# One change in five places of a two-block transformer kernel: the first weights sent by pairs of input tiles, the output projection of the gated-linear layer computed with tokens in rows, residual sums on VectorE, and fewer dummy products

## Chip, core and metric

The kernel runs on one core of a Trainium2 chip. The time is the device time of one execution, in microseconds (us); smaller is better. Engines are named as in the profile: PE is TensorE (the matrix engine), PEld its weight loads, DVE is VectorE, ACT is ScalarE, POOL is GpSimd, SP is the engine that issues the loads.

## What is computed

A sequence of 256 tokens of width 1024, in float32, passes through two blocks. Cut to what matters here:

```
c_act = silu(c)
mod = c_act @ w_ada + b_ada;  sh1, sc1, g1, sh2, sc2, g2 = split(mod, 6)
h = rmsnorm(x, norm_g[0]) * (1 + sc1) + sh1
y = hybrid_mixer(h, w_in, ...)               # 3 small attentions, gates, w_out
x = x + g1 * rmsnorm(y, norm_g[1])           # norm "n2"
h = rmsnorm(x, norm_g[2]) * (1 + sc2) + sh2  # norm "n3"
y = conv_ffn(h)                              # w_up, conv, gelu, w_down
x = x + g2 * rmsnorm(y, norm_g[3])           # norm "n4"

y = gla_mixer(x, ...)                        # gated-linear attention; its last step is  ... @ gla_w_out
x = layer_norm(ALPHA * x + y, ln_g[0], ln_b[0])      # norm "n5"
k, v = shared_kv(x, w_kv)
y = dilated_mixer(x, swa_w_in, swa_w_out, k, v)      # its last step is  ... @ swa_w_out
x = layer_norm(ALPHA * x + y, ln_g[1], ln_b[1])      # the output
```

## The kernel before

**Chunks.** All weights are cut into chunks of 2048 numbers per partition (1 MB; some are smaller), numbered in the order of use: QC, QI, KK, MISC, QA ... VB, ZG (12), BRANCH (3), WOUT (4), UP (22), DOWN (12), GK (2), GA, GQ (2), GV (4), GG (4), GOUT (4), SK (3), SV (3), SWA (16), SOUT (4). GOUT is `gla_w_out`, SK and SV are `w_kv`, SOUT is `swa_w_out`. SP issues the loads in the order of the list `STREAM` into four buffers `raw`; a load waits until the chunk four places ahead of it in the ring is used.

**Splitting.** A float32 product is made of three products in a shorter format (`three`): ACT rounds a chunk to its high part (`high`, whi), DVE subtracts it for the low part (`low`, wlo), and PE multiplies high by high, high by low and low by high. Activations are split in the same way (hhi/hlo, gohi/golo, ohi/olo). A chunk takes 48 such products of 256 columns. The split parts have three slots (`c % SPL`), and results have three PSUM banks (`res`, `bank(r)`); a bank is free when the engine that `drainer_of` names has read it.

**Layout.** Activations lie with features on the partitions and tokens in the columns (8 tiles of 128 features by 256 tokens). `fm` computes a chunk in that layout, `tm` with tokens on the partitions. `fm_first` interleaves two chunks over the input tiles k, so that it can start when the first tile of a freshly made activation is there; it needs the splits of both chunks.

**The start.** The first three chunks (QC, QI, KK) are not split: `direct` multiplies float32 as it is. They are loaded one chunk at a time between the eight parts of `w_ada` that the first norm needs (`ada`: a product and sum on DVE, two instructions for each part). `ADA_FIRST` fixes the order 0, 4, 1, 5, 2, 6, 3, 7. When parts j and 4 + j are done, DVE makes `pcol` for two tiles, ACT makes these two tiles of `tb` (the normed input), and PE may multiply them. The last tiles so wait for part 7. Then ACT splits chunks MISC and QA (`high(DIRECT)`, `high(DIRECT + 1)`), and copies the result QC in four pieces (`swap`); DVE rotates it (`rope`, m_qc), which frees the PSUM bank that chunk MISC needs.

**The norms n2, n3 and n4.** PE multiplies squares by a matrix of 1/1024 (`sums`, `last_squares`: its result is the mean on all partitions). ACT makes a first value of the root (`norm_guess`), for which `load_root` has loaded its table, and DVE improves it (`norm_rstd`) and scales y. The sums x + y go in four pairs of tiles in the order `PAIRS`; the second pair is summed on POOL (`add_pair`), the others on DVE. In n4 the first low part follows the third pair (`low_pair`). Meanwhile PE runs dummy products (`warm(n)`), the last before GK with n = 36.

**Norm n5.** Chunks GOUT to GOUT + 3 are computed by `fm_first` and `fm`, DVE adds the residual `xe` (x times ALPHA in another order of tokens, made early by POOL), PE forms means twice (`shift_mean`, `rest_mean`) and the mean of squares, DVE and ACT make the normed tiles one by one, and `fm_first` multiplies SK and SK + 1.

**The end.** For SOUT the residual is brought in by PE: sixteen products of x with the identity (`residual`), twelve of them before the first product of SOUT; for these PE waits for three free banks. ACT copies each result with a sum over its row (`accum_out`) and then squares it; DVE norms the rows and SP stores them.

## Time and profile before

| | |
|---|---|
| time, median of 3 runs (lowest, highest) | 786.86 us (785.42, 787.11) |
| the profiled execution: its time, its span | 786.95 us, 785.2 us |
| PE busy | 751.5 us, 96% of the span |
| DVE busy | 528.7 us, 67% |
| ACT busy | 394.9 us, 50% |
| POOL busy | 121.3 us, 15% |
| granted PE clock, mean | 0.987 |

The span runs from the first to the last instruction of the profiled execution, and its time holds 1.75 us beside it. Busy PE time counts the dummy products too, so 96% doesn't say that PE did useful work for all of it. In a row of the timeline the first number is the start in us from the span's start, the second how long the row's instructions took together, and in brackets stands how long the engine was idle before it and what ended that. PE records a float32 product as two instructions. In a row of the windows stand the stretch and its length, then the busy us of PE, PEld, DVE, ACT and POOL with the number of instructions in brackets, the granted PE clock (1.00 is the full 2.4 GHz, 0.50 is 1.2 GHz), the share of the DMA engines' time, and GB/s.

### The profile page before, as it was taken

How to read it: one execution, taken by the hardware profiler on the slowest of the kernel's cores; microseconds unless marked ns; L12 is line 12 of the kernel's file. 1: busy time of each engine (PE TensorE's matmuls, PEld its weight loads, DVE VectorE, ACT ScalarE, POOL GpSimd, SP SyncE). 2: the span in 40 equal slices, each digit the busy share in tenths (PEclk: the TensorE clock that was granted, in tenths of full speed). 3: DMA queues.
4: the chain of work that ended last, by engine and by line, in shares of the span. 5: the costliest groups of instructions: out<-in, count | busy, mean ns of one | idle time of the engine just before them, and what ended most of it. 6: DMA issues, size and time to landing. Idle time of an engine off the chain costs nothing. (4 is left out here: it accounts for less than half of the span.)

```text
span 785.2 us, 14371 instructions
## 1 busy us (share of the span) xinstructions
PE 751.5 (96%) x6044; PEld 732.4 (93%) x6044; DVE 528.7 (67%) x770; ACT 394.9 (50%) x555; POOL 121.3 (15%) x100
## 2 busy tenths in 40 slices
PE   8899989999898999999999999999989999999996
PEld 7889889899897999999999999999989999999995
DVE  5879978765868687778656556926685556556544
ACT  4195454555353555454444347627445555555633
POOL 0040000000521100000002150000025655333000
PEclk9999999999999999999999999979999999999999
DMA  8975575464355356554565524523437653333101
GB/s 355 417 291 215 215 268 187 190 259 171 108 177 199 115 208 210 173 200 157 209 247 210 211 90 180 184 88 108 145 124 246 201 185 135 134 109 119 44 1 54
DMA packets 20954, 140.10 MB, mean 178 GB/s; under 512 B 2357, under 2 KB 2997, under 8 KB 4890
## 3 DMA queue, kind: packets, MB, share of 16 engines
q1 hardware_dynamic: 20458, 137.28, 48.2%
q0 software_dynamic: 432, 1.90, 0.7%
q8 instruction: 48, 0.79, 0.4%
q14 instruction: 16, 0.13, 0.0%
HBM read 138.12 MB, written 1.05 MB: 177 GB/s over the span
## 5 line engine op out<-in xcount | busy, mean ns | idle before, releaser
L1593 PE MATMUL res<-hhi,whi 128*128 128x256 f32 (+1 forms) x1120 | 322.9, 288 | 5.3 <-DVE hlo L1071 2.9
L1035 DVE TENSOR_TENSOR wlo<-raw,whi 128x2048 fp32r<-128x2048 f32 (+3 forms) x102 | 230.0, 2256 | 142.9 <-ACT whi L647 138.3
L1595 PE MATMUL res<-hlo,whi 128*128 128x256 f32 (+1 forms) x1120 | 317.8, 284 | 0.0
L1594 PE MATMUL res<-hhi,wlo 128*128 128x256 f32 (+1 forms) x1120 | 317.8, 284 | 0.0
L647 ACT ACTIVATE whi<-raw 128x2048 fp32r<-128x2048 f32 (+3 forms) x102 | 190.1, 1865 | 132.5 <-issue 100.2
L1593 PEld LDWEIGHTS res<-hhi,whi 128*128 128x128 f32 (+1 forms) x1120 | 214.6, 192 | 7.2 <-issue 5.5
L1594 PEld LDWEIGHTS res<-hhi,wlo 128*128 128x128 f32 (+1 forms) x1120 | 214.4, 191 | 0.3
L1595 PEld LDWEIGHTS res<-hlo,whi 128*128 128x128 f32 (+1 forms) x1120 | 214.3, 191 | 0.2
L559 POOL TENSOR_TENSOR sq<-sq 128x512 f32<-128x512 f32 x6 | 14.9, 2482 | 293.7 <-ACT sq L853 168.5
L1593 PE MATMUL res<-uhi,whi 128*128 128x256 f32 x176 | 49.3, 280 | 1.0 <-ACT y L854 1.0
L1594 PE MATMUL res<-uhi,wlo 128*128 128x256 f32 x176 | 49.2, 280 | 0.0
L1595 PE MATMUL res<-ulo,whi 128*128 128x256 f32 x176 | 49.2, 280 | 0.0
L531 POOL TENSOR_TENSOR sq<-sq,rope 128x512 f32<-128x512 f32 x18 | 37.9, 2105 | 63.6 <-ACT sq L662 63.6
L1048 DVE CUSTOM_DVE_ANT_0 raw<-raw,cact,cols 128x1024 f32<-128x1024 f32 x32 | 41.8, 1343 | 0.0
L1593 PE MATMUL res<-whi,hhi 128*128 128x256 f32 x144 | 41.0, 285 | 0.0
L1594 PE MATMUL res<-whi,hlo 128*128 128x256 f32 x144 | 40.7, 283 | 0.0
L1595 PE MATMUL res<-wlo,hhi 128*128 128x256 f32 x144 | 40.7, 283 | 0.0
L1593 PEld LDWEIGHTS res<-uhi,whi 128*128 128x128 f32 x176 | 33.1, 188 | 1.2 <-ACT y L854 1.2
L784 ACT ACTIVATE up<-shared,unmax 128x128 f32<-128x128 f32 (+1 forms) x24 | 10.9, 456 | 45.0 <-DVE unmax L1186 45.0
L575 POOL TENSOR_TENSOR y<-y,sq 128x512 f32<-128x512 f32 x8 | 10.5, 1344 | 147.0 <-DVE sq L1214 147.0
L1594 PEld LDWEIGHTS res<-uhi,wlo 128*128 128x128 f32 x176 | 33.1, 188 | 0.0
L1595 PEld LDWEIGHTS res<-ulo,whi 128*128 128x128 f32 x176 | 33.1, 188 | 0.0
(331 smaller groups left out, 1242.0 us busy)
## 6 DMA issues: line engine op xcount, KB each, us to landing
raw<-in_wts SPq DMA_DIRECT2D x97, 1024.0 KB, 4.9
raw<-in_w_ada SPq DMA_DIRECT2D x16, 1024.0 KB, 4.9
shared<-in_w_ada SPq DMA_DIRECT2D x6, 1024.0 KB, 12.6
gates<-in_wts SPq DMA_DIRECT2D x3, 1024.0 KB, 15.4
raw<-in_wts SPq DMA_DIRECT2D x4, 768.0 KB, 7.3
y<-in_w_ada SPq DMA_DIRECT2D x2, 1024.0 KB, 10.3
x<-in_xT SPq DMA_DIRECT2D x2, 512.0 KB, 4.5
ln_rows<-in_ln_rows POOLq DMA_DIRECT2D x1, 1024.0 KB, 7.9
```

The source lines that it names most:

```text
L531: nc.gpsimd.tensor_tensor(xsw, xsw, table[:, 1:2, :].to_broadcast([P, 2, T]), ALU.mult).then_inc(sin_done, 1)
L559: nc.gpsimd.tensor_tensor(sq[:, 0:2, :], sq[:, 0:2, :], sq[:, a:a + 2, :], ALU.add).then_inc(presummed, 1)
L575: nc.gpsimd.tensor_tensor(y[:, 2 * j:2 * j + 2, :], y[:, 2 * j:2 * j + 2, :], gtmp[:, n % 4, :].rearrange("p (a b) -> p a b", a=2), ALU.ad ...
L647: nc.scalar.activation(hi[:, 0:kt * w], raw[RAW_OF["w", c] % RAW][:, 0:kt * w], ACT.Copy).then_inc(hi_ready, 1)
L784: nc.scalar.activation(up[:, s % 3, 0:nk], usc[:, s % 2, 0:nk], ACT.Exp, scale=-1.0, bias=unmax[:, s % 4:s % 4 + 1], accum_out=uden[:, s % ...
L1035: nc.vector.tensor_tensor(lo[:, 0:b], raw[RAW_OF["w", c] % RAW][:, 0:b], hi[:, 0:b].bitcast(f32), ALU.subtract).then_inc(lo_ready, 1)
L1048: nc.vector.tensor_tensor_reduce(out=w[:, D * i:D * i + D], in0=w[:, D * i:D * i + D], in1=cact[:, :], op0=ALU.mult, op1=ALU.add, scale=1. ...
L1593: mm(out, ah, bh, start=first, stop=False)
L1594: mm(out, al, bh, start=False, stop=False)
L1595: return mm(out, ah, bl, start=False, stop=last)
```

## The change

1. `STREAM`: the three direct chunks are sent as four loads ("rows"), each with two input tiles of all three chunks: 0.75 MB in pieces of 2 KB (before: 1 MB in pieces of 8 KB). The fourth stands behind part 7 of `w_ada`. PE takes the direct products in that order, with 4 dummies between.
2. n2 and n4: all four sums on DVE. In n2 part 19 of `w_ada` is worked on after the sums and not ahead of them; `load_root` stands one chunk earlier. In n4 each low part follows the next pair of y. In DOWN, `load_root` stands at the first chunk. The dummies before GK are 24 and not 36.
3. GOUT and n5: tokens lie in rows. PE adds the residual by sixteen products of `xe` with the identity, computes result after result for token tile t = 0 and then t = 1, and each tile is normed in rows as the end of the kernel is; PE transposes it (`hidden`), and ACT and DVE split it. Chunk GOUT + 3 has a buffer of its own (wgo). SK is computed by `fm`, not by `fm_first`. POOL loads the two rows of the norm (1 MB) into gv.
4. SOUT: the residual is added by DVE as it reads the bank, with the row sums; PE's sixteen products with the identity are gone, and the first product needs two free banks.

```diff
-    if GOUT <= c < SV or SWA <= c < SWA + 12:
+    if SK <= c < SV or SWA <= c < SWA + 12 or c >= SOUT:
         return "dve"
...
-    STREAM += [("ada", _i), ("ada", 4 + _i)] + [("w", _i)] * (_i < DIRECT)
+    STREAM += [("ada", _i), ("ada", 4 + _i), ("rows", _i)]
...
-            return SOUT - 1 if c == NC - 1 else c - SPL
+            return {NC - 1: SOUT - 1, SK - 1: GOUT - 1, SK + 2: GOUT}.get(c, c - SPL)
...
+                if kind == "rows":
+
+                    a, m = P * 512 * DIRECT * n, 512 * DIRECT
+                    dst = gates[:, :, :].rearrange("p (c k) n -> p c (k n)", c=DIRECT)[:, :, 512 * n:512 * n + 512]
+                    sp.dma_start(dst, wts[a:a + P * m].rearrange("(p c n) -> p c n", p=P, c=DIRECT)).then_inc(direct_full[n], 16)
...
-                    add_pair("n2")
...
-                    add_pair("n4")
...
+                if c - 1 == GG:
+                    pool.wait_ge(o_done, 2)
+                    pool.dma_start(gv[:, :, :], ln_rows5_d).then_inc(rows5_in, 16)
+                if SV <= c - 1 < SV + 2:
+                    t = c - 1 - SV
+                    pool.wait_ge(h_transposed, 4)
+                    nc.gpsimd.tensor_scalar(x_rows[:, t, :], x_rows[:, t, :], ALPHA, None, ALU.mult).then_inc(x_ready, 1)
...
+                if b == GOUT:
+                    ps = result(FIRST_RESULT[b])
+                    for t in range(2):
+                        row_sum(ps[:, T * t:T * t + T], t, 0, T, 0).then_inc(drained_act if t else act_self, 1)
+                    act_count[0] += 1
+                    load_root()
+                if b == GOUT + 1:
+                    row_sum(result(FIRST_RESULT[b])[:, 0:T], 0, T, T, 1).then_inc(drained_act, 1)
+                    act.wait_ge(z_shift, 1)
+                    row_squares(z[:, 0, 0:512], 0, 0, 3).then_inc(z_squared, 1)
+                if b == GOUT + 2:
+                    ps = result(FIRST_RESULT[b])
+                    row_sum(ps[:, :], 0, 512, 512, 2).then_inc(z_summed, 1)
+                    row_squares(ps[:, :], 0, 512, 4).then_inc(drained_act, 1)
+                    row_root(0, 0)
+                if b == GOUT + 3:
+                    row_sum(result(FIRST_RESULT[b])[:, 0:T], 1, T, T, 1).then_inc(drained_act, 1)
+                    act.wait_ge(z_shift, 2)
+                    row_squares(z[:, 1, 0:512], 1, 0, 3).then_inc(z_squared, 1)
+                    high(SK)
+                    hidden_high(0)
+                    ps = result(FIRST_RESULT[b] + 1)
+                    row_sum(ps[:, :], 1, 512, 512, 2).then_inc(z_summed, 1)
+                    row_squares(ps[:, :], 1, 512, 4).then_inc(drained_act, 1)
+                    row_root(1, 0)
+                    hidden_high(1)
+                    high(SK + 1)
...
-                if b + 2 in ADA_AFTER and b != WOUT:
+                if b + 2 in ADA_AFTER and b not in (WOUT, UP - 2):
                     ada(ADA_AFTER[b + 2])
...
-                            if i == 1 and k % 2:
-                                ins.then_inc(y_scaled[n], 1)
-                            else:
-                                own(ins)
-                        if i != 1:
-                            nc.vector.tensor_tensor(x[:, 2 * j:2 * j + 2, :], x[:, 2 * j:2 * j + 2, :],
-                                                    y[:, 2 * j:2 * j + 2, :], ALU.add).then_inc(scaled[n], 1)
-                        if n == "n4" and i == 2:
-                            low_pair(0)
+                            own(ins)
+                        if n == "n4" and i:
+                            low_pair(i - 1)
+                        nc.vector.tensor_tensor(x[:, 2 * j:2 * j + 2, :], x[:, 2 * j:2 * j + 2, :],
+                                                y[:, 2 * j:2 * j + 2, :], ALU.add).then_inc(scaled[n], 1)
...
+                def hidden_low(t):
+                    for i in range(2):
+                        dve.wait_ge(h_hi, 2 * t + i + 1)
+                        ks, ts = slice(4 * i, 4 * i + 4), slice(t * P, t * P + P)
+                        nc.vector.tensor_tensor(hlo[:, ks, ts], (pS, pT)[t][:, 512 * i:512 * i + 512].rearrange("p (k n) -> p k n", k=4),
+                                                hhi[:, ks, ts].bitcast(f32), ALU.subtract).then_inc(h_lo, 1)
...
+                if b == GOUT + 3:
+                    dve.wait_ge(drained_act, RESULT_DRAIN[FIRST_RESULT[b]][1])
+                    shift_of(1)
+                    low(SK)
+                    hidden_low(0)
+                    rows_normed(1, 0, gv, x_rows, x_rows_ready)
+                    hidden_low(1)
+                    low(SK + 1)
+
+                def row_add(ps, t, a, n, at):
+                    return nc.vector.tensor_tensor_reduce(out=z[:, t, a:a + n], in0=ps, in1=x_rows[:, t, a:a + n], op0=ALU.add,
+                                                          op1=ALU.add, scale=1.0, scalar=0.0, accum_out=zs[:, t, at:at + 1])
...
+            for j in range(4):
+                for c in range(DIRECT):
+                    direct(c, j)
+                if j < 3:
+                    warm(4, meanw)
...
-                        warm(36)
+                        warm(24)
...
+                    if c == GOUT + 1:
+                        for t in range(2):
+                            ps = bank(r + 1 + 2 * t)
+                            residual(ps, 0, t, (2, 3))
+                            wh, wl = weights(GOUT + 1)
+                            for k in range(KT):
+                                last = token_product(ps, 0, t, k, gohi, golo, wh, wl, False, k == KT - 1)
+                            last.then_inc(product_done, 1)
+                            ps = bank(r + 2 + 2 * t)
+                            residual(ps, 0, t, range(4, KT))
+                            for d in range(2):
+                                wh, wl = weights(GOUT + 2 + d)
+                                for k in range(KT):
+                                    last = token_product(ps, T * d, t, k, gohi, golo, wh, wl, False, d == 1 and k == KT - 1)
+                                if t == 1 and d == 0:
+                                    hidden(0)
+                            last.then_inc(product_done, 1)
+                        warm(16, ident, pX[:, 0:P])
+                        hidden(1)
...
-                            fm_first(c, hhi, hlo, lambda k: pe.wait_ge(*in_low("n5", k)), ARRIVAL)
-                        elif c > SK + 1:
+                            fm(c, hhi, hlo, None, lambda k: pe.wait_ge(h_lo, 3 + k // 4))
+                        else:
...
-                        pe.wait_ge(x_ready, KT)
-                        first = [bank(r + d) for d in range(3)]
-                        for d in range(2):
-                            for t in range(2):
-                                residual(first[d], T * t, t, (2 * d, 2 * d + 1))
-                        residual(first[2], 0, 0, range(4, KT))
+                        first = [bank(r + d) for d in range(2)]
```

**PE, the direct products** (`res<-tb,gates`; the rows with meanw are dummies). Before:

```order
L1641 MATMUL pS<-meanw 128x128 x16
L1820 MATMUL res<-tb,gates 128x256 x4
L1641 MATMUL pS<-meanw 128x128 x8
L1820 MATMUL res<-tb,gates 128x256 x4
L1641 MATMUL pS<-meanw 128x128 x8
L1820 MATMUL res<-tb,gates 128x256 x40
```

Now:

```order
L1634 MATMUL pS<-meanw 128x128 x16
L1817 MATMUL res<-tb,gates 128x256 x12
L1634 MATMUL pS<-meanw 128x128 x4
L1817 MATMUL res<-tb,gates 128x256 x12
L1634 MATMUL pS<-meanw 128x128 x4
L1817 MATMUL res<-tb,gates 128x256 x12
L1634 MATMUL pS<-meanw 128x128 x4
L1817 MATMUL res<-tb,gates 128x256 x12
```

The 48 direct products are the same, now in four equal groups, one for each pair of tiles; 12 dummies stand between them in place of 16.

**DVE, norms n2 and n3** (the rows with raw, mod and cact are the two instructions of part 19 of `w_ada`). Before:

```order
L1048 ISA raw,mod<-raw,cact,cols 128x1024
L1048 ISA mod 128x1
L1048 ISA raw,mod<-raw,cact,cols 128x1024
L1048 ISA mod 128x1
L1280 TENSOR_TENSOR pcol<-mod,cols 128x8
L1281 SCALAR_TENSOR_TENSOR pcol<-mod,cols 128x8
L1059 SCALAR_TENSOR_TENSOR logvar<-rstd 128x256
...
L1289 SCALAR_TENSOR_TENSOR y<-y,pcol,rstd 128x256 x4
L1296 TENSOR_TENSOR x<-x,y 128x512
```

Now:

```order
L1283 TENSOR_TENSOR pcol<-mod,cols 128x8
L1062 SCALAR_TENSOR_TENSOR logvar<-rstd 128x256
...
L1290 SCALAR_TENSOR_TENSOR y<-y,pcol,rstd 128x256 x2
L1295 TENSOR_TENSOR x<-x,y 128x512
L1054 ISA raw,mod<-raw,cact,cols 128x1024
L1054 ISA mod 128x1
L1054 ISA raw,mod<-raw,cact,cols 128x1024
L1054 ISA mod 128x1
L1302 SCALAR_TENSOR_TENSOR pcol<-mod,cols 128x8
L1062 SCALAR_TENSOR_TENSOR logvar<-rstd 128x256
```

Part 19 moved from ahead of the root of n2 to behind the last of four sums, ahead of the root of n3.

**ACT, GOUT to SK.** `res<-` results are read from the banks; hhi is the split input of SK. Before:

```order
L647 ACTIVATE whi<-raw 128x2048 x3
L936 ACTIVATE sq<-tb 128x512 x2
L647 ACTIVATE whi<-raw 128x2048
L936 ACTIVATE sq<-tb 128x512
L667 ACT_TABLE_LOAD
L667 ACTIVATE one<-cols 128x1
L936 ACTIVATE sq<-tb 128x512
L676 ACTIVATE rstd<-logvar,cols 128x256
L684 ACTIVATE hhi<-tb,cols 128x256 x8
```

Now, from the sum over the rows of t = 1 on (ACT's part of `b == GOUT + 3`):

```order
L692 ACTIVATE tb,zs<-res 128x256
L696 ACTIVATE sq,zs<-tb,zs 128x512
L634 ACTIVATE whi<-raw 128x2048
L706 ACTIVATE hhi<-pS 128x4x128 x2
L692 ACTIVATE tb,zs<-res 128x512
L696 ACTIVATE sq,zs<-res,zs 128x512
L700 ACTIVATE zs<-zs,cols 128x1
L706 ACTIVATE hhi<-pT 128x4x128 x2
L634 ACTIVATE whi<-raw 128x2048 x3
```

The split of chunk SK and of the first token tile stand ahead of the sum of the last result, and the split of the second token tile comes after the whole of its norm.

## Rows read from the trace of the kernel before

**Rows 1.** Windows, 510 to 525 us: busy time of each engine, granted clock, DMA

```profile
510.00:525.00 15.00, 15.00 (x129) 14.11 (x129) 3.06 (x18) 1.20 (x2) 0.00 (x0) 0.68 0.31 123
```

**Rows 2.** Timeline, 25 to 47 us: start, length, engine, line, operation

```profile
25.06 0.43 SPq L483 DMA_DIRECT2D rope<-in_rope  x1
25.53 1.85 SPq L506 DMA_DIRECT2D raw<-in_wts  x4
...
33.18 1.28 DVE L1048 CUSTOM_DVE_ANT_0 shared<-shared,cact,cols 128x1024 f32<-128x1024 f32 x1 [1.69 <-DMA shared<-in_w_ada]
...
40.69 2.47 ACT L647 ACTIVATE whi<-raw 128x576 fp32r<-128x576 f32 x2
...
46.58 0.31 PE L1593 MATMUL res<-hhi,whi 128*72 128x256 f32 x1 [0.48 <-DVE m_qc L1103]
```

**Rows 3.** DMA issues, 25 to 27.5 us: count, KB each, median us to landing

```profile
raw<-in_wts SPq DMA_DIRECT2D x3, 1024.0 KB, 15.8
raw<-in_wts SPq DMA_DIRECT2D x1, 288.0 KB, 11.8
rope<-in_rope SPq DMA_DIRECT2D x1, 256.0 KB, 11.5
```

**Rows 4.** Timeline, 232 to 255 us (norms n2 and n3)

```profile
233.97 1.28 ACT L667 ACT_TABLE_LOAD   x1
...
236.14 1.13 PE L1692 MATMUL pX<-sq,meanw 128*128 128x256 f32 x4 [1.32 <-ACT sq L814]
236.19 1.28 DVE L1048 CUSTOM_DVE_ANT_0 raw<-raw,cact,cols 128x1024 f32<-128x1024 f32 x1
...
239.11 0.42 DVE L1059 SCALAR_TENSOR_TENSOR logvar<-rstd 128x256 f32<-128x256 f32 x1
...
240.49 1.00 DVE L1289 SCALAR_TENSOR_TENSOR y<-y,pcol,rstd 128x256 f32<-128x256 f32 x2
...
242.14 2.80 DVE L1289 SCALAR_TENSOR_TENSOR y<-y,pcol,rstd 128x256 f32<-128x256 f32 x4
...
249.70 0.42 DVE L1059 SCALAR_TENSOR_TENSOR logvar<-rstd 128x256 f32<-128x256 f32 x1 [2.39 <-ACT rstd L676]
```

**Rows 5.** Timeline, PE in the second group of DOWN

```profile
399.05 0.39 PE L1593 MATMUL res<-uhi,whi 128*128 128x256 f32 x1 [1.02 <-ACT y L854]
```

**Rows 6.** Timeline, 444 to 453 us (norm n4)

```profile
444.53 8.20 PE L1641 MATMUL pS<-ident 128*128 128x128 f32 x72
...
447.73 0.69 DVE L1296 TENSOR_TENSOR x<-x,y 128x512 f32<-128x512 f32 x1
...
451.78 0.68 DVE L1088 TENSOR_TENSOR hlo<-x,hhi 128x512 fp32r<-128x512 f32 x1
```

**Rows 7.** Timeline, 550 to 587 us (GOUT, n5, first product of SK)

```profile
550.68 0.36 PE L1593 MATMUL res<-gohi,whi 128*128 128x256 f32 x1 [0.21 <-DVE wlo L1035]
...
555.94 0.69 DVE L1080 TENSOR_TENSOR golo<-y,gohi 128x512 fp32r<-128x512 f32 x1 [0.70 <-ACT gohi L931]
...
573.11 2.29 DVE L1035 TENSOR_TENSOR wlo<-raw,whi 128x2048 fp32r<-128x2048 f32 x1 [1.12 <-ACT whi L647]
...
586.09 0.36 PE L1593 MATMUL res<-hhi,whi 128*128 128x256 f32 x1 [2.21 <-DVE hlo L1071]
```

**Rows 8.** Windows, 586 to 612.2 us: products of SK and later, without a gap

```profile
586.00:612.20 26.20, 26.11 (x218) 26.14 (x219) 16.71 (x18) 14.97 (x17) 14.12 (x12) 1.00 0.55 192
```

**Rows 9.** Timeline, 727 to 785 us (SWA, SOUT and the last norm)

```profile
727.76 0.66 PE L1770 MATMUL pT<-ident,dp 128*128 128x128 f32 x4 [0.48 <-DVE dp L1534]
...
750.85 2.92 PE L2002 MATMUL res<-ident,x 128*128 128x128 f32 x24 [1.27 <-ACT sgs L981]
...
777.49 0.60 ACT L959 ACTIVATE tb<-res 128x512 f32<-128x512 f32 x1 [3.66 <-PE res L1595]
778.21 0.21 DVE L1501 TENSOR_SCALAR zs<-zs 128x1 f32<-128x1 f32 x1 [2.02 <-ACT tb L959]
781.27 1.41 DVE L1517 SCALAR_TENSOR_TENSOR y<-sq,zs,ln_rows 128x512 f32<-128x512 f32 x2
```

335 lines of the change are left out of this document (132 added, 203 removed).

## The prediction, made before the changed kernel ran

> **What bounds the kernel now.** I began with the page's shares (PE busy 96% of the span) and read the waits of PE, because a busy PE leaves two ways to save: products that need not be there, and waits. The dummies count as busy, so a wait can hide behind them. Then I read the timeline of all engines around each edited place. Most of the run is PE at full rate: between 586 and 612.2 us, 218 products take 26.2 us, 0.120 us each at full clock [rows 8]. What the change can move are six places, and at each the reader should look for the row that ends PE's wait.
>
> The profiled execution took 786.95 us, a span of 785.2 and 1.75 beside it; the median of the three runs is 786.86, so nothing has to be scaled. The sum is made against 786.95.
>
> **Start: −1.3 us.** The loads are bound by the queue. SP issues four raw chunks from 25.53 on, one each 0.47 us [rows 2]. The 288 KB one lands 11.8 us after its issue, at 37.3, and the three of 1 MB have a median of 15.8, so the middle one (issued at 26.5) lands at 42.3 [rows 3]: the two large ones between take about 2.5 us each. Thus 1 MB costs 2.47 us, 0.425 MB per us. Ahead of part 3 of `w_ada` there are now three loads of 0.75 MB instead of three of 1 MB; 0.75 MB less is 1.8 us. DVE waits 1.69 us for its parts at 33.18 [rows 2], so `pcol` and the last tiles of tb come about 1.8 us earlier. PE's direct products are four groups of 5.2 us, the last from about 37.8 to 43, and are not the bound. But ACT's splits of MISC and QA, begun at 40.69 and 2.47 us long together (by their 576 and 2048 columns 0.54 and 1.93), need QA's landing, and the bytes ahead of QA are unchanged: 37.3 + 2.5 = 39.8. Split to 41.7; from the end of the splits (43.16) to MISC's first product (46.58) is 3.42 us of swaps and rope [rows 2]; so it comes at 45.1, 1.5 us earlier. I take −1.3, since pieces are shorter. Bounds: −1.9 (tiles' gain whole) and +0.3. For the pieces, the nearest row: rope was issued at 25.06 and landed 11.5 later, at 36.56 [rows 2, 3]; the 288 KB chunk, which has pieces of 2.3 KB, landed 0.77 later, 0.38 MB per us and so 10% slower than the large ones. On 3 MB that is 0.8 us.
>
> The Trainium skill, "Perfetto Trace Analysis", section "DMA Optimizations", says that larger transfers use the memory's bandwidth better and advises to merge pieces of 2 KB into 4 or 8 KB; this change does the reverse. It names no figure. If the rule holds at this size, what the 288 KB row prices would come off the start's gain: an estimate by page and row of 775.7 us in place of 774.9.
>
> **Norms n2 and n3: −2.5 us.** ACT loads the root's table at 233.97 for 1.28 us (and 0.2 for its first use) just ahead of the square of the last result, and PE waited 1.32 us for that square at 236.14 [rows 4]. The load moves one chunk earlier, where ACT idles. DVE is free from 236.19, when it takes part 19 of `w_ada`: until its root of n2 at 239.11 go 2.9 us [rows 4]. With mean and guess about 1.4 us earlier, and part 19 behind the sums, the root starts at 236.5 (−2.6). The root takes 1.38 (239.11 to 240.49). A pair of y takes 1.04 with its start, a sum 0.61; while POOL adds its pair, two pairs of y take 2.80 rather than 2.0, so the shared sum cost DVE 0.75 [rows 4]: four sums on DVE (6.6 us) end at 244.5, which is no more than three plus that loss. Now part 19 (two of 1.28, 2.5 with all) stands ahead of the root of n3. There DVE used to wait 2.39 us for square, mean and guess, from 247.31 to 249.70 [rows 4]. The cover is almost whole: 244.5 + 2.5 + 0.2 = 247.2, while the guess would be there at 246.9. So n3's root moves from 249.70 to 247.2, −2.5. Bounds: −2.8 (no remainder), and −1.5, if the guess is known no earlier than it is now. The load that waits for part 19 in the ring starts some 8 us later; its chunk is needed some 20 us later. The dummies here end before the waits and stay.
>
> **DOWN: −1.0 us.** PE waits 1.02 us at 399.05 for ACT's y [rows 5], which stood behind the same table load. Earlier in DOWN ACT has room of about 3 us. Bounds: 0 and −1.0.
>
> **Norm n4: −2.6 us.** PE runs 36 dummies (72 instructions) from 444.53, 8.20 us, to 452.73; the first low part ends at 451.78 + 0.68 = 452.46, so the dummies are the bound by 0.3 [rows 6]. Now: first sum ends at 448.42; while ACT rounds it (0.7), DVE makes the next pair of y (1.0), and the low part follows, to 450.1. 24 dummies take 5.47 us, to 450.0. The first product of GK moves from 452.73 to 450.1. The later low parts follow each some 2.3 us (a pair of y, a sum, a low part), to 452.3, 454.6, 456.6; PE's 96 products for two chunks need them no sooner than 453.0, 455.9 and 458.8. Bounds: −2.7, and −2.0 if each handoff takes 0.2 longer.
>
> **GOUT and n5: +0.1 us.** Now 35.4 us pass from 550.68 to SK's first product at 586.09, with 2.21 us of wait at its end [rows 7]. After: 192 products of 0.120 are 23.1 us [rows 8]; sixteen identity products, priced by the 24 instructions (twelve products) that took 2.92 us [rows 9], 3.8; a wait of 0.9 in the middle, because the last golo ends at 555.94 + 0.69 = 556.63 [rows 7] and t = 0 wants it at 555.75; eight transposes 1.3, at 0.66 for four [rows 9]. So the last result stands at 579.6. ACT sums it while DVE finishes the split of SK (2.29, as at 573.11 [rows 7]) and the low part of t = 0. By the kernel's own end, DVE starts 0.7 after ACT's copy (777.49 to 778.21) and normed rows are written 4.5 us later, at 781.27 + 1.41 = 782.68 [rows 9]: start at 580.3, rows at 584.8, their first half at 584.1. Four transposes (0.66), ACT's rounding (0.6), DVE's low part (0.7): SK's first product at 586.2 against 586.09. So a shorter tail pays for longer PE work and no more. Bounds: −1.5 (the split of SK off the path, transposes hidden), +2.5.
>
> **SOUT: −4.7 us.** PE waits 1.27 us at 750.85 for the third bank, and then has twelve identity products, 2.7 us to the next start, and four later, 0.97 [rows 9]. All go: the first product at 749.6, 192 products to 772.6 instead of 777.46, −4.9. The tail gets a DVE sum in place of ACT's copy of 0.60 [rows 9]; DVE's sum of equal size takes 0.69 [rows 6], and reading its row sum about 0.1: +0.15. Bounds: −4.9 and −3.5 (the second bank late by 1.3).
>
> **Sum:** −1.3 − 2.5 − 1.0 − 2.6 + 0.1 − 4.75 = −12.05; 786.95 − 12.05 = **774.9 us**.
>
> **Rivals.**
> *The long handoff in GOUT.* ACT has the split of SK, the rounding of t = 0 and then the sum of the last result in one queue, and DVE likewise; PE's transposes of t = 0 stand inside t = 1's products. For it: three engines wait in turn; tile 0 has only 1.8 us of room (normed at 573.5, wanted 575.3). Against: most steps take durations that rows show. If the norm of t = 0 is 2 us late and t = 1's again, +4: 779 us.
> *The start gives nothing.* QA's split stays the bound, with shorter pieces: 776.2 us.
> *The change doesn't do what it says.* Behind n2, n4, the start and DOWN the next wait (a weight split, a load) is as late as before, and takes the 7.4 us back. Only SOUT remains, with nothing behind it but the tail: 782.3 us. Against: from 586 to 612 PE has no gap, and DMA is busy only 0.55 of the time [rows 8].
> *The clock falls: slower.* From 510 to 525 us PE was busy for all of 15.00 us with small products of the attention and the granted clock was still 0.68 [rows 1], a mean between 2.4 and 1.2 GHz: busy time alone does not keep it up. GOUT now holds sixteen identity products and sixteen transposes of 128 columns, and 12 dummies fewer stand before GK. At 1.2 GHz a product of 0.120 takes at most 0.24. To end above 788.5 (slower by 0.2%) takes 13.6 us, 113 products, a little over half of four chunks' 192, all at the low level. Against: between 727 and 755 us identity products and transposes of the same shape took 0.12 and 0.165 [rows 9], without a fall. With only GOUT and SK low for 15 us the loss is 7.5 and the time 782.
>
> The Trainium skill, "TensorE: Matmul & The Clock Gate", section "Part 4: PE-mode transpose", says that transposes do not count as PE work in the same way for the clock. By it the stretch of the hidden tiles would be the place of such a fall, and the time 782 us; the row at 727.76 shows the price of transposes and not what the clock makes of them, so no row of before settles it.
>
> **How the numbers follow.** Forecast 0.65, handoff 0.11, start 0.11, swallowed gains 0.05, clock 0.08. The measurement tells 0.2%, 1.6 us. All but the clock case are faster by more; of it 0.05 is slower and 0.03 within 0.2%: 0.92, 0.03, 0.05. The forecast's lower end takes −1.5 in GOUT, −0.6 at the start, −0.5 from n2, n4 and SOUT together, and 1 us for what runs differ: 771.3. The upper end takes in the handoff and start together (774.9 + 1.3 + 4 = 780.2). Range: 771.0 to 780.5.
>
> **What would show it.** Right: MISC's first product near 45.2; n3's root at 246 (by the start's and its own shift: 249.7 − 1.3 − 2.5); no wait for ACT's y in DOWN; GK's first product some 7.4 us before 452.73; the distance from GOUT's first to SK's first product near 35.5; 192 products of SOUT without identity products, and from the last one to the end 7.9 us. Wrong: a granted clock under 1 behind 525 us, a wait of over 1 us at SK's first product beyond DVE's chain, part 19 as releaser of n3's root by more than 0.3 us, or parts of `w_ada` landing no earlier than before. The weakest terms are GOUT, where four bounded handoffs follow each other, and the start.

## The result, and the profile after

The changed kernel takes 774.82 us (median of 4 runs, 773.84 to 775.20) against 786.34 us (785.42 to 787.11) of the kernel before, run beside it: ratio 0.9852, 95% interval 0.9835 to 0.9869. The forecast was 774.9, counted from the profiled execution of before (786.95): a gain of 12.05, where the medians show 11.5 and the two profiled executions 11.75 (786.95 and 775.20). One more execution of the changed kernel, in its second series below, took 1202.17 us at a mean granted clock of 0.559 and is left out of every median and ratio. The profiled execution has a span of 773.4 us. The page's lines of PE and of the granted clock:

```profile
span 773.4 us, 14293 instructions
PE 742.9 (96%) x6004; PEld 725.5 (94%) x6004; DVE 523.3 (68%) x783; ACT 394.5 (51%) x556; POOL 107.6 (14%) x87
PEclk9999999999999999999999999979999999999998
```

PE's share is 96% as before. So the share tells nothing of a change of 12 us; the waits at single places do. Here is the timeline of the changed kernel at the places of the prediction's six terms, in order of time:

```profile
31.66 1.28 DVE L1054 CUSTOM_DVE_ANT_0 shared<-shared,cact,cols 128x1024 f32<-128x1024 f32 x1 [1.21 <-DMA shared<-in_w_ada]
...
40.33 1.91 ACT L634 ACTIVATE whi<-raw 128x2048 fp32r<-128x2048 f32 x1 [0.49 <-DMA raw<-in_wts]
...
45.66 0.31 PE L1586 MATMUL res<-hhi,whi 128*72 128x256 f32 x1 [1.94 <-DVE m_qc L1106]
...
233.16 0.43 DVE L1062 SCALAR_TENSOR_TENSOR logvar<-rstd 128x256 f32<-128x256 f32 x1 [0.80 <-ACT rstd L659]
...
241.12 1.28 DVE L1054 CUSTOM_DVE_ANT_0 raw<-raw,cact,cols 128x1024 f32<-128x1024 f32 x1
...
243.85 0.42 DVE L1062 SCALAR_TENSOR_TENSOR logvar<-rstd 128x256 f32<-128x256 f32 x1
...
246.92 0.36 PE L1586 MATMUL res<-hhi,whi 128*128 128x256 f32 x1 [0.97 <-DVE hlo L1074]
...
392.08 0.28 PE L1586 MATMUL res<-uhi,whi 128*128 128x256 f32 x1
...
437.62 5.52 PE L1634 MATMUL pS<-ident 128*128 128x128 f32 x48
...
443.30 0.36 PE L1586 MATMUL res<-hhi,whi 128*128 128x256 f32 x1 [0.16 <-DVE hlo L1091]
...
548.69 0.39 PE L1586 MATMUL res<-whi,gohi 128*128 128x256 f32 x1 [1.08 <-DVE golo L1083]
...
575.86 1.32 PE L1704 MATMUL pT<-ident,x 128*128 128x128 f32 x8 [1.28 <-DVE x L1462]
578.02 0.55 PE L1586 MATMUL res<-hhi,whi 128*128 128x256 f32 x1 [0.84 <-DVE hlo L1469]
...
742.68 0.28 PE L1586 MATMUL res<-whi,ohi 128*128 128x256 f32 x1
...
765.66 0.69 DVE L1491 CUSTOM_DVE_ANT_0 tb<-res,x 128x512 f32<-128x512 f32 x1 [0.29 <-PE res L1588]
...
769.53 1.42 DVE L1462 SCALAR_TENSOR_TENSOR y<-sq,zs,ln_rows 128x512 f32<-128x512 f32 x2
```

A row says something only against the same row of before, and a late start carries everything ahead of it. So the start of a row is not compared, but the distance between two marked rows. The marks are the first product of MISC, of WOUT, of UP, the last of DOWN, the first of GK, of GOUT, of SK, of SOUT, and the end of the last normed half (us; the third row is a second profile of the same code, below):

| | to MISC | to WOUT | to UP | DOWN's last | to GK | to GOUT | to SK | to SOUT | to the end |
|---|---|---|---|---|---|---|---|---|---|
| before | 46.58 | 164.12 | 42.08 | 189.80 | 10.05 | 98.07 | 35.41 | 167.43 | 29.16 |
| changed | 45.66 | 161.79 | 39.47 | 188.74 | 7.64 | 99.00 | 35.72 | 164.65 | 28.27 |
| changed again | 45.72 | 163.42 | 39.47 | 188.75 | 7.64 | 97.83 | 35.71 | 163.37 | 28.26 |
| forecast of the difference | −1.3 | 0 | −2.5 | −1.0 | −2.6 | 0 | +0.1 | −4.0 | −0.8 |

Two kinds of columns stand side by side. Five repeat to 0.02 us in both profiles of the changed kernel: UP, DOWN, GK, SK, end; MISC differs by 0.06. Three differ by over 1 us in the same code: WOUT, GOUT and SOUT. To read SOUT, the windows of the changed kernel around SK's first product help (columns as in [rows 1]):

```profile
574.00:576.00 2.00, 0.72 (x7) 0.53 (x6) 1.86 (x6) 0.10 (x1) 0.00 (x0) 1.00 0.91 379
576.00:578.00 2.00, 1.17 (x8) 0.71 (x8) 1.28 (x3) 1.38 (x3) 0.00 (x0) 0.87 1.05 428
578.00:580.00 2.00, 1.98 (x9) 2.00 (x10) 0.89 (x2) 2.00 (x2) 0.00 (x0) 0.50 0.77 324
580.00:584.00 4.00, 4.00 (x32) 4.00 (x31) 4.00 (x2) 1.41 (x1) 0.00 (x0) 0.89 0.24 39
```

From 577.5 to 580.9 us the granted clock is 0.50, that is 1.2 GHz, and 9 products fit into 2 us, which hold 17 at 0.120 each: some 1.3 us lost at SK (164.65 against 163.37 us from SK to SOUT). Nothing like it stood there before. The second profile of the same code has 1.00 in all these windows, with the same two waits:

```profile
576.00:578.00 2.00, 1.31 (x8) 0.84 (x8) 1.28 (x3) 0.88 (x2) 0.00 (x0) 1.00 1.05 412
578.00:580.00 2.00, 1.48 (x12) 1.51 (x13) 1.04 (x2) 2.00 (x2) 0.00 (x0) 1.00 0.90 377
```

GOUT differs by the stretch of [rows 1]. Before, the low clock lasted 10.2 us there, from 509.3 to 519.6; in the first profile of the changed kernel it lasted 13.7, from 499.0 to 512.6; in the second 10.2 again. The window of before and that of the changed kernel:

```profile
508.00:520.00 12.00, 12.00 (x121) 11.11 (x121) 5.02 (x19) 0.00 (x0) 0.00 (x0) 0.57 0.49 176
...
496.00:514.00 18.00, 17.76 (x172) 16.45 (x172) 7.73 (x21) 2.40 (x2) 0.00 (x0) 0.62 0.38 139
```

In all fourteen profiles GK to GOUT takes 98.9 to 99.0 us where that stretch lasts 13.7 (four of them) and 97.6 to 98.1 where it lasts 10.2.

### The profile page after: what moved, and what is told of

It reads as the page before. It is cut to its first block, busy times and chain, and to the rows that moved or that the text cites. A ratio compares the mean times of both kernels' runs of the same rounds, so it can differ in the third digit from the quotient of the medians.

```text
span 773.4 us, 14293 instructions
## 1 busy us (share of the span) xinstructions
PE 742.9 (96%) x6004; PEld 725.5 (94%) x6004; DVE 523.3 (68%) x783; ACT 394.5 (51%) x556; POOL 107.6 (14%) x87
## 4 chain that ended last, share of the span: by engine, by line
PE 61%; DVE 20%; issue 9%; ACT 6%; DMA 3%; SPq 1%; POOL 0%; DVEq 0%; ACTq 0%
PE res L1586 18%; PE res L1588 17%; PE res L1587 17%; DVE wlo L1041 5%; ACT whi L634 4%; DVE raw L1054 3%; DMA raw<-in_wts 2%; PE pX L1777 2%; PE pX L1957 1%; PE pS L1757 1%; DMA y<-in_w_ada 1%; DVE shared L1054 1%; ACT sq L649 1%; PE pT L1767 1%; DVE y L1290 1%
## 5 line engine op out<-in xcount | busy, mean ns | idle before, releaser
L1041 DVE TENSOR_TENSOR wlo<-raw,whi 128x2048 fp32r<-128x2048 f32 (+3 forms) x101 | 226.9, 2248 | 146.4 <-ACT whi L634 142.0
L555 POOL TENSOR_TENSOR sq<-sq 128x512 f32<-128x512 f32 x4 | 10.7, 2677 | 181.2 <-ACT sq L855 167.4
## 6 DMA issues: line engine op xcount, KB each, us to landing
shared<-in_w_ada SPq DMA_DIRECT2D x6, 1024.0 KB, 11.5
```

The source lines that it names most:

```text
L555: nc.gpsimd.tensor_tensor(sq[:, 0:2, :], sq[:, 0:2, :], sq[:, a:a + 2, :], ALU.add).then_inc(presummed, 1)
L1041: nc.vector.tensor_tensor(lo[:, 0:b], raw[RAW_OF["w", c] % RAW][:, 0:b], hi[:, 0:b].bitcast(f32), ALU.subtract).then_inc(lo_ready, 1)
```

## The experiments

All times are medians, and each ratio is to the kernel before in runs of the same series. Since a fall of the clock is worth as much as most terms, each verdict is read first from the distances of the profile and then from the time; where the time lies outside the range that was expected, the text says so. "Theory A" and "rival B" are those of the expectation just above. Line numbers in rows are those of each kernel's own text.

### The changed kernel again

No edit.

> The changed kernel once more, to see what differs between executions of the same code. Theory A: the stretches at a low granted clock, the wait at WOUT's first product and the landing of the fifth part of w_ada differ from execution to execution, while the distances between marked instructions that the change moves stay within 0.05 us: 2.6 from n2's mean to UP under before, 2.40 from n4's root to GK, GOUT to SK 0.3 over before. The time is 774.8 us (774.2 to 775.4). Rival B: these are fixed by the code; then this trace has the fall at 578 us and none at 84 or 106 us, as the first had.

773.94 us, ratio 0.9848 (0.9835 to 0.9860), 0.3 below the range of A. Theory A holds for the distances. Here products are 0.21 us apart from 83 to 90 us, where the first profile has 0.12; at SK it is the reverse. The WOUT column has two more causes of its kind. Before had the clock low near 107 us. And PE waited 0.94 us for WOUT's first low part. Two rows of the timeline of before, and its window around 107 us:

```profile
208.73 4.10 DVE L1275 SCALAR_TENSOR_TENSOR hlo<-y,hhi 128x512 fp32r<-128x512 f32 x3
210.69 0.36 PE L1593 MATMUL res<-hhi,whi 128*128 128x256 f32 x1 [0.94 <-DVE hlo L1275]
```

```profile
106.00:112.00 6.00, 6.00 (x37) 5.90 (x38) 4.60 (x12) 3.19 (x6) 0.00 (x0) 0.72 0.62 217
```

Three such DVE instructions take 4.10 us (1.81, 1.77 and 0.68) where one alone takes 0.69; POOL's additions run beside them (four from 206.24, 5.45 us in all). DVE's first and POOL's third start within 0.02 us of each other, and one of the two is slow: here DVE's with 1.81, in the first profile of the changed kernel POOL's with 1.81 in place of 1.28, while DVE's first takes 0.69 and its next 1.63. The three instructions just before, which read a result bank beside POOL's first two additions, take 0.69 as alone. In some profiles DVE's first low part is slow and PE waits 0.95 (before, 36 dummies, parts 1 and 2, products for transposes, changed again, filled waits); in the others a later one is, and PE does not wait. MISC to WOUT takes 162.9 us in the one kind and 161.7 in the other, as long as the clock does not fall near 107 us, and falls near 85 not at all or for 3.4 us only.

### Part 1 undone

```diff
-    STREAM += [("ada", _i), ("ada", 4 + _i), ("rows", _i)]
+    STREAM += [("ada", _i), ("ada", 4 + _i)] + [("w", _i)] * (_i < DIRECT)
...
-                pe.wait_ge(direct_full[j], 16)
+                pe.wait_ge(direct_full[c], 16)
```

> The changed kernel with part 1 undone: the direct chunks are loaded one by one in pieces of 8 KB and multiplied in the old order. In the changed kernel MISC's first product starts at 45.66 us, 0.92 earlier than before, but the trace gains another 2.3 us up to the first square of n2 (231.42 against 236.14, with no edit between). Theory A: the further gain belongs to the start: the earlier phase avoids a low granted clock at 107 to 111 us and collisions of POOL and DVE near 208 us. Then MISC's first product is back near 46.5, the clock falls again near 107 us, the first square of n2 stands near 234.6 and the time is 774.8 + 3.2 = 778.0 us (776.9 to 778.5). Rival B: the start is worth what stands at MISC and the rest is chance of a run: 774.8 + 0.9 = 775.7 us (775.2 to 776.2).

774.68 us, ratio 0.9862 (0.9847 to 0.9876): neither. The distance MISC to WOUT is 161.72, as in the changed kernel, so A's further gain does not belong to the start. For MISC itself one must compare profiles that began alike. DVE takes up the third part of `w_ada` near 18.6, 20.0 or 21.4 us, with the same code, and no landing sets this: it follows the first norm without a wait for DMA in all fourteen profiles, and in the later two groups that norm waits for PE's mean. What differs is how long PE runs at half pace at the start. The same 24 dummy instructions in the changed kernel and in the next experiment's (part 19 ahead of the sums), and DVE's wait there:

```profile
5.90 2.94 PE L1634 MATMUL pS<-meanw 128*128 128x128 f32 x24
...
7.69 5.49 PE L1632 MATMUL pS<-meanw 128*128 128x128 f32 x24
...
17.65 0.42 DVE L1062 SCALAR_TENSOR_TENSOR logvar<-rstd 128x256 f32<-128x256 f32 x1 [2.88 <-ACT rstd L659]
```

They are 0.21 us apart at first in every profile and 0.11 later; 0.11 is reached by 6.3 us in seven profiles, near 10.6 in three and past 12.9 in four. The records of the granted clock say 1.00 in all this time, so they do not show it. At 20.0 there are this kernel and, with part 1 in place, those with products for transposes and with filled waits. This kernel:

```profile
32.93 1.28 DVE L1052 CUSTOM_DVE_ANT_0 shared<-shared,cact,cols 128x1024 f32<-128x1024 f32 x1 [1.51 <-DMA shared<-in_w_ada]
...
46.32 0.31 PE L1584 MATMUL res<-hhi,whi 128*72 128x256 f32 x1 [1.33 <-DVE m_qc L1104]
```

and with part 1 (products for transposes):

```profile
31.64 1.28 DVE L1054 CUSTOM_DVE_ANT_0 shared<-shared,cact,cols 128x1024 f32<-128x1024 f32 x1 [0.18 <-DMA shared<-in_w_ada]
...
45.67 0.31 PE L1586 MATMUL res<-hhi,whi 128*72 128x256 f32 x1 [1.47 <-DVE m_qc L1106]
```

The part lands 1.29 us earlier and MISC starts 0.65 earlier. At 18.6 us the pair before and changed gives 0.92. At 21.4 us, in four profiles with part 1, DVE never waits for a landing and MISC starts at 46.1 to 46.3; no profile without part 1 began so late, so what it is worth there is not known. So part 1 is worth 0.65 to 0.9 us where loads are waited for; by the time, it is not told from nothing.

### Part 19 ahead of the sums

```diff
-                if b + 2 in ADA_AFTER and b not in (WOUT, UP - 2):
+                if b + 2 in ADA_AFTER and b != WOUT:
...
-                    ada(ADA_AFTER[UP])
```

> The changed kernel with part 19 of w_ada worked on ahead of n2's sums, as before; the table load stays early and all sums on DVE. Theory A: DVE, free at 232.3, is busy with part 19 until 234.85, so n2's root starts at 234.9 in place of 233.16 and the last sum ends 1.7 us later; but behind it the root of n3 waits only for square, mean and guess (2.4 us) instead of part 19 and pcol (2.7), so n3's root and the time are 1.4 us later: 776.2 us (775.8 to 776.6). Rival B: the move itself was worth the whole 2.6 of the norms (the early table load nothing): 777.4 us (777.0 to 777.8).

775.11 us, ratio 0.9866 (0.9852 to 0.9881). WOUT to UP is 41.16 against 39.47, 1.7 us more, and 42.08 before:

```profile
232.75 1.27 DVE L1054 CUSTOM_DVE_ANT_0 raw<-raw,cact,cols 128x1024 f32<-128x1024 f32 x1
...
235.68 0.43 DVE L1062 SCALAR_TENSOR_TENSOR logvar<-rstd 128x256 f32<-128x256 f32 x1
...
246.11 0.43 DVE L1062 SCALAR_TENSOR_TENSOR logvar<-rstd 128x256 f32<-128x256 f32 x1 [2.39 <-ACT rstd L659]
```

The wait of 2.39 is back ahead of n3's root. Theory A is right in kind: of the 2.6 us, the move has 1.7 (1.4 expected), which leaves 0.9 for the early table load and the sums together; the table load was not undone by itself. The time shows 0.3 to 1.2 of it and lies 0.7 below A's range; this profile has no fall at SK, and the loss of one is as large as what is sought.

### The second sum on POOL

```diff
+                    add_pair("n2")
...
+                    add_pair("n4")
...
+                        if i != 1:
```

> The changed kernel with the second of the four sums x + y in n2 and n4 on POOL, as before; part 19, the table loads, the order of low parts and the dummies stay as changed. Theory A: in n2 DVE saves a sum (0.61 us) and pays 0.75 because POOL's addition slows the y beside it, so n2's root to n3's root stays within 0.2 us of 10.7 (in the changed kernel), and n3's root waits for part 19 as before. In n4 the low part of the second pair waits for POOL's sum (1.44 us) and ACT, but the low part that the first product needs does not: n4's root to GK stays 4.9, later products wait some tenths. 774.7 us (774.2 to 775.2). Rival B: four sums on DVE are most of what part 2 gave; 2 us or more come back: 776.6 us or more.

773.14 us, ratio 0.9829 (0.9814 to 0.9843). Theory A by the distances. n2's root to n3's root is 0.16 us longer and n4's root to GK 0.13 shorter than in the changed kernel (4.77 against 4.90). DVE's four y beside POOL's addition:

```profile
236.83 2.80 DVE L1303 SCALAR_TENSOR_TENSOR y<-y,pcol,rstd 128x256 f32<-128x256 f32 x4
```

that is the 2.80 of [rows 4], as against two times 1.00 without POOL (DVE's pair at 240.49 there). "All sums on DVE" is worth nothing by itself; the order of work around the sums is. The median lies 1.1 us below A's range and 0.8 below that of the changed kernel's second series, which no distance of the profile explains (its end of the last half is at 770.25, against 770.15 in the second profile). The intervals of the two ratios overlap (0.9814 to 0.9843, 0.9835 to 0.9860); I take it for the scatter of executions, which is not shown.

### 36 dummies before GK

```diff
-                        warm(24)
+                        warm(36)
```

> The changed kernel with 36 dummies before GK instead of 24. Theory A: the 24 end at 443.14 and the first low part at 443.16, so both bind alike, and twelve more are all on the path: 12 x 0.23 = 2.7 us, 777.5 us (777.0 to 778.0), and GK's first product near 445.9. Rival B: the later low parts (the last ends at 449.7) bind behind them, part of the delay is taken back, 1.3 us or less remain: 776.1 us or less. The granted clock near 499 to 513 us is to be read too: the stretch at the low level was 1.3 us dearer after than before, and here it starts 2.7 us later.

778.05 us, ratio 0.9896 (0.9880 to 0.9913). To GK 9.91 us against 7.64:

```profile
439.26 8.20 PE L1634 MATMUL pS<-ident 128*128 128x128 f32 x72
447.21 0.36 PE L1586 MATMUL res<-hhi,whi 128*128 128x256 f32 x1
```

The dummies are the bound again, and the product behind them waits for nothing. They cost 2.27 of the 2.7 us that twelve take. The rest was a wait in the changed kernel: with 24, GK's first product starts 0.43 us behind the start of the last dummy, here 0.03. GK to GOUT is 97.91, as in the second profile of the changed kernel (97.83), so nothing is taken back: A. The low clock on that way lasts 10.2 us here, and with 24 dummies in eight of twelve profiles, so the number of dummies does not set it.

### The table load late in DOWN

```diff
-                if b == DOWN:
-                    load_root()
...
+                    if j == 0:
+                        load_root()
```

> The changed kernel with the root's table loaded ahead of DOWN's first results, as before. Theory A: PE waits 1.0 us again for ACT's y at DOWN's second group (in the changed kernel there is no wait at 392.08) and nothing later takes it back: 774.8 + 1.05 = 775.9 us (775.6 to 776.1). Rival B: the wait is taken back where PE waits anyway, in the norm n4 or in GLA: 774.8 us (774.5 to 775.1).

774.88 us, ratio 0.9865 (0.9850 to 0.9880). By the time alone it would be B. The profile says A: UP to DOWN's last is 190.02 against 188.74, +1.28, all behind is as in the changed kernel, and PE's wait is back:

```profile
391.38 1.28 ACT L654 ACT_TABLE_LOAD   x1
...
393.62 0.39 PE L1586 MATMUL res<-uhi,whi 128*128 128x256 f32 x1 [1.01 <-ACT y L856]
```

Four runs from 773.70 to 776.54 cannot show 1.3 us. This profile had no fall at SK, which alone makes up for it against the first profile of the changed kernel.

### SOUT's residual on PE

```diff
-                        first = [bank(r + d) for d in range(2)]
+                        pe.wait_ge(x_ready, 2)
+                        first = [bank(r + d) for d in range(3)]
+                        for d in range(2):
+                            for t in range(2):
+                                by_identity(first[d], T * t, t, (2 * d, 2 * d + 1))
+                        by_identity(first[2], 0, 0, range(4, KT))
```

> The changed kernel with the residual of SOUT brought in by PE again: sixteen products of the scaled rows of x with the identity, twelve ahead of SOUT's first product behind three free banks, and ACT sums the results. Theory A: the wait for the third bank (1.2), twelve products (2.7) and four (1.0) come back, less 0.15 in the tail: 774.8 + 4.8 = 779.6 us (779.2 to 779.9). Rival B: the wait was a matter of the phase and does not come back: 778.3 us.

779.18 us, ratio 0.9907 (0.9892 to 0.9922), at the lower bound of A's range:

```profile
744.13 2.92 PE L1700 MATMUL res<-x,ident 128*128 128x128 f32 x24 [1.27 <-ACT sgs L993]
```

The row is that of before [rows 9], wait and all. SK to SOUT's first product takes 4.06 us more than in the first profile of the changed kernel (both with a fall at SK), and the way from there to the end 0.95 more.

### Parts 1 and 2 alone

The kernel before with those hunks of the diff above.

> The kernel before with parts 1 and 2 alone: GOUT, n5 and SOUT as before. Theory A: part 3 gives nothing between GOUT's first and SK's first product (35.3 against 35.4 us) and costs 1.2 us right behind, where the granted clock is at 1.2 GHz from 578 to 581 us; part 4 gives 4.9. So this kernel is 4.9 - 1.2 + 0.1 = 3.8 us above the changed one: 778.6 us (778.0 to 779.2), with SK's first products at 0.12 us each. Rival B: the low clock has nothing to do with part 3 and shows here as well: 774.8 + 4.9 = 779.8 us (779.4 to 780.2).

778.83 us, ratio 0.9903 (0.9890 to 0.9916). GOUT to SK is 35.40, SK to SOUT 167.44 with the clock at 1.00: as before. The numbers fit A (778.6), but four of the eight profiles with part 3 and no edit between GOUT and SK (changed again, part 19 first, second sum on POOL, table late) have no fall there either. So A's 1.2 us is a matter of some executions, and A's sum is right in part by luck.

### Who brings the clock down ahead of SK

Three kernels. More dummies:

```diff
-                        warm(16, ident, pX[:, 0:P])
+                        warm(21, ident, pX[:, 0:P])
                         hidden(1)
+                        warm(3, ident, pX[:, 0:P])
```

> The changed kernel with 21 dummies in place of 16 ahead of the transposes of the second token tile, and 3 behind them, so that PE's two waits before SK (1.28 and 0.84 us) are filled. Theory A: the idle time and its like bring the clock down from 578 to 581 us; filled, the products of SK take 0.12 us from the first on, and 1.2 us are gained: 773.6 us (773.2 to 774.0). Rival B: it is the transposes that PE runs there, or what lies further back; the clock falls all the same, and the time stays at 774.8 (774.4 to 775.2) or 0.2 more, if a dummy is late.

Products instead of transposes:

```diff
-                        last = nc.tensor.transpose((pS, pT)[t][:, P * k:P * k + P], x_rows[:, t, P * k:P * k + P], ident[:, :])
+                        last = mm((pS, pT)[t][:, P * k:P * k + P], x_rows[:, t, P * k:P * k + P], ident[:, :], start=True, stop=True)
```

> The changed kernel with the sixteen transposes of the hidden tiles done as plain float32 products with the identity. A product of 128x128 takes 0.24 us where a transpose takes 0.165. Theory A (the waits bring the clock down): the clock falls as it does in the changed kernel; the first eight products lie in PE's wait, four of the last are on the path and cost 0.3: 775.1 us (774.8 to 775.4). Rival B (the transposes bring it down, since they do not count as PE's work for the clock): SK's products take 0.12 us from the first on, 1.2 us are gained: 773.9 us (773.5 to 774.2).

No dummies: `warm(16, ident, pX[:, 0:P])` left out.

> The changed kernel without the sixteen dummies between GOUT's last product and the second tile's transposes: PE stands still for some 4.8 us there. Theory A (PE's idle time brings the granted clock down): a fall at SK in every execution, at least as long as the one of 12 products, so at least 1.2 us over an execution without a fall: 775.0 to 776.5 us, and SK to SOUT at 164.65 us or more in the trace against 163.4 without a fall. Rival B (the transposes, or chance): SK to SOUT as in the others, 163.4 or 164.65, and the time 774.8 (774.2 to 775.4).

The times are 774.36 (0.9845, 0.9832 to 0.9858), 774.40 (0.9848, 0.9835 to 0.9860) and 777.16 us (0.9884, 0.9872 to 0.9897). The first two lie between the ranges of A and B, so they decide nothing by the time. Their profiles have no fall at SK, but that proves little where four of eight without any edit there have none; and the dummies by themselves leave GOUT to SK at 35.68. The third one tells, and costs more than A expected (776.5 at most). Its windows, and two rows of its timeline:

```profile
566.00:571.00 5.00, 4.97 (x43) 4.77 (x41) 2.44 (x2) 3.49 (x5) 0.00 (x0) 1.00 0.00 0
571.00:574.00 3.00, 0.00 (x0) 0.00 (x0) 2.83 (x9) 1.59 (x5) 1.59 (x3) 1.00 0.69 218
574.00:576.00 2.00, 0.17 (x1) 0.18 (x2) 1.86 (x6) 0.06 (x1) 0.00 (x0) 0.51 0.94 383
...
580.00:584.00 4.00, 4.00 (x21) 4.00 (x20) 3.74 (x2) 2.03 (x2) 0.00 (x0) 0.50 0.19 27
```

```profile
575.83 1.97 PE L1704 MATMUL pT<-ident,x 128*128 128x128 f32 x8 [4.85 <-DVE x L1462]
578.45 0.55 PE L1586 MATMUL res<-hhi,whi 128*128 128x256 f32 x1 [0.65 <-DVE hlo L1469]
```

PE stands still from 571.0, and the clock is low from 574.1 to 584.3, from before the first transpose of the second tile. With the sixteen dummies it is at 1.00 from 574 to 576 in both profiles of the changed kernel. The eight transposes of the first tile ran at 567.1, as they do in the changed kernel, so the idle time is what this kernel adds: a wait of 4.85 us is enough to bring the clock down. That the 1.28 and 0.84 us of the changed kernel do so is not shown. The price: GOUT to SK is 36.16 in place of 35.71 (the transposes take 1.97 in place of 1.32), SK to SOUT is 165.95 in place of 163.37, 3.0 us together; the time shows 2.3 to 3.2. Whether transposes do something besides stays open: the kernel with products in their place had no fall (one profile). These products cost more than I expected, 1.25 us in place of 0.3 from GOUT to SK: I had the first tile's eight lie in a wait, and they stand among the products of t = 1, where every 0.1 us delays the last result (they take 1.95 in place of 1.04).

### The waits filled

```diff
                         for k in range(KT):
+                            if k == 6:
+                                residual(bank(r + 1), 0, 0, (2, 3))
+                                residual(bank(r + 2), 0, 0, range(4, KT))
                             pe.wait_ge(go_lo, k // 2 + 1)
...
                     row_sum(result(FIRST_RESULT[b])[:, 0:T], 1, T, T, 1).then_inc(drained_act, 1)
+                    high(SK)
...
                     row_squares(z[:, 1, 0:512], 1, 0, 3).then_inc(z_squared, 1)
-                    high(SK)
```

and the 21 and 3 dummies.

> The changed kernel with three waits around GOUT filled: the six identity products of the second and third result are issued while PE waits for the last golo (1.08 us there now); ACT splits SK's chunk before the squares of t = 1, so that DVE's norm of t = 1 waits for nothing but the last result (0.3 us); 21 and 3 dummies ahead of SK in place of 16. Theory A: GOUT to SK becomes 1.05 + 0.3 = 1.35 us shorter, 34.4 us, and with no fall of the clock at SK the time is 774.8 - 1.4 - 0.6 (half of the executions had the fall of 1.2) = 772.8 us (772.2 to 773.6). Rival B: the last result is not the bound at GOUT's end; DVE's queue is, and 34.4 stays 35.7: 774.2 us.

772.54 us (772.35 to 773.58), ratio 0.9829 (0.9816 to 0.9841), in A's range and the fastest of the study beside 773.14. GOUT to SK is 34.22, 1.50 us less than in the changed kernel (expected 1.35), with the clock at 1.00 behind; the three edits were not run one by one:

```profile
547.39 1.50 PE L1696 MATMUL res<-ident,xe 128*128 128x128 f32 x12
...
574.30 1.32 PE L1704 MATMUL pT<-ident,x 128*128 128x128 f32 x8
575.46 0.83 PE L1634 MATMUL pX<-ident 128*128 128x128 f32 x6
576.46 0.36 PE L1586 MATMUL res<-hhi,whi 128*128 128x256 f32 x1 [0.17 <-DVE hlo L1469]
```

The six identity products take the place of the 1.08 us wait, and PE has no wait of over 0.2 us left from GOUT to SK.

## Why the prediction was right

The total was hit to 0.1 us, partly by luck. In the distances the terms that I forecast sum to −11.6 as measured (−12.05 forecast), and three things that I did not forecast sum to −0.1, of which none is small. That the median of before beside the run is 0.6 below the profiled execution from which I counted helped too.

**Start, forecast −1.3, measured −0.92.** The mechanism held: part 3 landed 1.5 us earlier (1.8 forecast), tiles ceased to bind, QA's landing did, as the ACT row with its wait for DMA shows. QA landed at 40.3 and not at 39.8. From 10 to 38 us the loads ran at 410 GB/s in four profiles with part 1 and at 418 and 419 in the two without: 2% slower, some 0.5 to 0.6 us on that stretch. But only 3 MB of the 11.5 MB of the stretch come in pieces of 2 KB, and if they alone are slower, they cost 7 to 8% more, an estimate; the bound from the 288 KB row (10%, 0.8 us) was near. The Trainium skill, "Perfetto Trace Analysis", section "DMA Optimizations", has the sign right: larger transfers are faster. Another error can weigh as much: I took one execution's start for the code's. In four of the twelve profiles with part 1 PE kept its half pace past 12.9 us, the first norm and all tiles came later, and the tiles bound again.

**n2 and n3, −2.5; measured −2.61.** n3's root comes behind part 19 and `pcol`, at 243.85, and its releaser is DVE itself; ACT's guess was there at 243.56, so 0.2 to 0.3 us of cover were missing (0.3 forecast). The share of it that "sums on DVE" has is nil, as costed.

**DOWN, −1.0; measured −1.06.** The wait at 392.08 is gone.

**n4, −2.6; measured −2.41.** The low part is ready at 443.15 and releases PE 0.16 us behind the dummies. Both bounds lie together, as worked out, and the handoff has its price.

**GOUT and n5, +0.1; measured +0.31.** This term was put together from a dozen durations, and each step stands where it was forecast, shifted: a wait of 1.08 for the last golo (0.9), the last result 28.7 us after GOUT's first product (28.9), the norm's 4.5 us, and then SK. DVE began that norm some 0.3 us behind ACT's sum, since it still had the low part of the first tile to make. The rival of the long handoff (+4) did not come: the first tile's transposes wait for nothing.

**SOUT, −4.75 in the sum; measured −2.78 − 0.89, and without the fall at SK −4.06 − 0.89 = −4.95.** The wait of the third bank, 1.27, did not move to the second one; with the identity products back on PE it came back to the hundredth.

**What was not forecast.** −2.3 between MISC and WOUT (a fall near 107 us, 1.2, and the wait at WOUT, 1.1, both of them in the profile of before and not in that of after), +0.9 between GK and GOUT (the fall at 509 us lasted 13.7 us and not 10.2) and +1.3 behind SK. All three come and go between executions of one code, or of kernels that are alike up to there. By the first of them two signs that I gave as times came 2 us early (n3's root at 243.85 for 246, GK's first product at 443.30 for some 445.3). That the clock might fall I had as a rival, with transposes as its place, and its sign, a granted clock under 1 behind 525 us, came. It fell at that place in four of eight profiles, for 3.4 us and not 15. What brings it down there stays open: PE waits 2.1 us in all there, in the profiles with a fall and in those without. The Trainium skill, "TensorE: Matmul & The Clock Gate", section "Part 4: PE-mode transpose", says that transposes do not count as PE work in the same way; no run here shows that, and in the kernel without dummies the clock fell 5.9 us behind the first tile's transposes and 1.8 ahead of the second's, with PE idle in between.

## What to carry to other kernels

Measure an edit of 1 us by the distance between two marked instructions around it, in two profiles of the same code, before the total is asked: five distances repeated to 0.02 us where the total scattered by 1 to 3, and the three that did not repeat each held a stretch of low clock or a collision. A wait is best filled with work that must be done anyway (the identity products), and dummies pay only up to the moment at which the data is there: twelve too many cost 2.3 us, sixteen too few 3.0. When two profiles are compared at their start, see first that they began alike. When an operation moves between engines, ask what else moved with it; here the order of work around the sums gave the time and the engine of the sums gave none.

## What was unexpected of the hardware

The same code loses 1.2 to 1.3 us to a stretch of 3.4 us at 1.2 GHz in one execution and not in the next, at 578 us; a stretch near 107 us, in the profile of before and in that of SOUT's residual on PE, costs 1.2 as well. The fall near 85 us costs nothing up to WOUT when it lasts 3.4 us (161.7 us from MISC to WOUT with it and without) and 0.6 in the two profiles in which it lasts 6.8. At the start PE keeps a spacing of 0.21 us for dummies that later take 0.11 until 6, 10.6 or 13 us, while the granted clock in the records is 1.00; the first norm comes 1.4 or 2.5 to 2.9 us later for it. And of a DVE instruction and a POOL addition that start within 0.02 us of each other one takes 1.8 us, in place of 0.69 or 1.28; when it is DVE's first low part, PE waits 0.95 us and the way to WOUT is 1.1 us longer.
